# The causal mask of the decays: a minimum on VectorE in place of two TensorE matmuls per row spread

## The reference, cut to what matters

```python
a_cum = jnp.cumsum(a_dt, axis=-1)
causal = jnp.tril(jnp.ones((SSD_CHUNK, SSD_CHUNK), dtype=bool))
decay = jnp.exp(jnp.where(causal, a_cum[..., :, None] - a_cum[..., None, :], -jnp.inf))
cb = jnp.einsum("bclgn,bcsgn->bgcls", cc, bc)
y_diag = jnp.einsum("bgecls,bcsgep->bclgep", cb[:, :, None] * decay, x)
```

## Time and profile before

| what | value |
|---|---|
| time, median of 3 runs | 1684.83 us (1681.4, 1684.83, 1687.41) |
| span of the profiled execution, first to last instruction | 1680.5 us |
| TensorE busy | 1591.5 us, 95% |
| VectorE busy | 1020.3 us, 61% |
| ScalarE busy | 843.9 us, 50% |
| GpSimd busy | 64.0 us, 4% |
| mean granted TensorE clock | 0.985 of full |
| bytes moved | 265.47 MB, 158 GB/s |

### The profile page before, as it was taken

How to read it: one execution, slowest core, us unless ns; L and a number is a source line. 1 busy time by engine, 2 the same in 40 slices (tenths; PEclk the granted TensorE clock), 3 DMA queues, 4 the chain that set the end, 5 groups by cost and what they waited for, 6 DMA issues and landing times.

```text
span 1680.5 us, 21488 instructions
## 1 busy us (share of the span) xinstructions
PE 1591.5 (95%) x8006; PEld 1329.4 (79%) x8006; DVE 1020.3 (61%) x1287; ACT 843.9 (50%) x940; POOL 64.0 (4%) x38
## 2 busy tenths in 40 slices
PE   5999999999999998999999999989999799879987
PEld 4988878788778886988888878778888688668876
DVE  5977765555564544777775655565453665666564
ACT  4556566454444443556666544354433545554463
POOL 0001100000000000010110000000000010001000
PEclk9999999999999999999999999999999899989999
DMA  5443444344445554443334444435555553436341
GB/s 198 154 171 129 149 154 164 133 154 148 170 162 189 187 183 144 151 175 132 144 129 172 151 151 151 150 128 207 195 179 183 194 189 112 157 113 223 113 165 66
DMA packets 39666, 265.47 MB, mean 158 GB/s; under 512 B 4343, under 2 KB 5400, under 8 KB 9112
## 3 DMA queue, kind: packets, MB, share of 16 engines
q1 hardware_dynamic: 37800, 260.41, 42.9%
q10 hardware_dynamic: 1776, 3.83, 0.6%
HBM read 262.39 MB, written 1.84 MB: 157 GB/s over the span
## 4 chain that ended last, share of the span: by engine, by line
PE 84%; DVE 5%; issue 5%; ACT 5%; DMA 1%; ACTq 0%; DVEq 0%; SPq 0%
PE ps L524 22%; PE ps L526 21%; PE ps L525 21%; PE ps L529 4%; PE ps L753 3%; PE ps L754 3%; PE ps L755 3%; ACT w_high L965 2%; DVE scratch L1326 2%; PE ps L634 2%; ACT w_high L1155 1%; PE ps L668 1%; DVE w_low L1326 1%; PE ps L609 1%; PE ps L607 1%
## 5 line engine op out<-in xcount | busy, mean ns | idle before, releaser
L1326 DVE TENSOR_TENSOR w_low<-w_raw,w_high 128x2048 fp32r<-128x2048 f32 (+2 forms) x252 | 559.4, 2226 | 530.6 <-ACT w_high L965 453.1
L965 ACT ACTIVATE w_high<-w_raw 128x2048 fp32r<-128x2048 f32 (+1 forms) x198 | 372.4, 1883 | 428.3 <-PE ps L526 416.3
L524 PE MATMUL ps<-w_high,u_high 128*128 128x512 f32 x1376 | 553.8, 402 | 9.8 <-DVE u_low L1326 5.2
L526 PE MATMUL ps<-w_high,u_low 128*128 128x512 f32 x1376 | 540.0, 392 | 0.0
L525 PE MATMUL ps<-w_low,u_high 128*128 128x512 f32 x1376 | 539.8, 392 | 0.0
L524 PEld LDWEIGHTS ps<-w_high,u_high 128*128 128x128 f32 x1376 | 260.8, 190 | 68.2 <-issue 9.1
L526 PEld LDWEIGHTS ps<-w_high,u_low 128*128 128x128 f32 x1376 | 260.6, 189 | 56.3
L525 PEld LDWEIGHTS ps<-w_low,u_high 128*128 128x128 f32 x1376 | 261.1, 190 | 53.1 <-issue 1.9
L524 PE MATMUL ps<-w_high,b_high 128*128 128x512 f32 x384 | 151.7, 395 | 1.9 <-issue 1.9
L526 PE MATMUL ps<-w_high,b_low 128*128 128x512 f32 x384 | 149.7, 390 | 0.0
L525 PE MATMUL ps<-w_low,b_high 128*128 128x512 f32 x384 | 149.5, 389 | 0.0
(11 more groups left out here) (222 smaller groups left out, 1400.4 us busy)
## 6 DMA issues: line engine op xcount, KB each, us to landing
w_raw<-in_stream SPq DMA_DIRECT2D x238, 1024.0 KB, 4.8
w_raw<-in_stream SPq DMA_DIRECT2D x10, 512.0 KB, 3.4
par<-in_pars SPq DMA_DIRECT2D x4, 265.0 KB, 4.9
h<-in_x SPq DMA_DIRECT2D x1, 1024.0 KB, 7.4
ple_gain<-in_ple_g ACTq DMA_DIRECT2D x2, 512.0 KB, 6.2
scratch<-rev ACTq DMA_DIRECT2D x2, 512.0 KB, 5.6
w_raw<-in_stream SPq DMA_DIRECT2D x4, 256.0 KB, 2.6
out<-h SPq DMA_DIRECT2D x2, 512.0 KB, 2.6
```

The costliest lines, as they stand in the source:

```text
L524: nc.tensor.matmul(o, hi, whi, start=start, stop=False, **kw)
L526: return nc.tensor.matmul(o, lo, whi, start=False, stop=stop, **kw)
L965: nc.scalar.activation(WH[:, c % RING, 0:n], W[:, c % RING, 0:n], ACT.Copy).then_inc(high_ready, 1)
L1326: return nc.vector.tensor_tensor(out=o, in0=a, in1=b, op=op)
```

## The change

The mask matmuls go, and with them the two matrices ident_r and never_r that GpSimd prepared at the start. The spread now sums all 128 rows of decay_rows, with weights that are one in the 64 rows of chunk t and zero in the others. VectorE then takes the minimum of the spread and the running sum of s into EM, and ScalarE takes the exponentials from EM to EM. Where l comes before s the running sum of l is the larger, the minimum is that of s, the exponential is 1, and cb's zero removes it. TensorE's waits for banks 6 and 7 (the state matmul and the off-diagonal product) are now for the minimum and not for the exponentials; VectorE takes over ScalarE's waits. Its minimum stands after the products of x at 2i+7 and, at 2i+9, after what the same chunk number holds for earlier groups.

```diff
@@ TensorE, at c = 2i+6 and 2i+8
-                            k = slice(t * 2 * HEADS, (t + 1) * 2 * HEADS)
-                            ones = tri_r[k, P - 1:P].to_broadcast([2 * HEADS, P])
+                            half_of = (tri_r, later_r)[t][:, P // 2 - 1:P // 2].to_broadcast([P, P])
                             for b in range(2):
-                                nc.tensor.matmul(four(ps[:, 6 + b, :]), ident_r[:, :], bc(never_r[:, :].unsqueeze(1), 4, P),
-                                                 start=True, stop=False)
-                                last = nc.tensor.matmul(ps[:, 6 + b, :], ones, DR[k, b * 512:(b + 1) * 512],
-                                                        start=False, stop=True)
+                                last = nc.tensor.matmul(ps[:, 6 + b, :], half_of, DR[:, b * 512:(b + 1) * 512],
+                                                        start=True, stop=True)
                             last.then_inc(row_ps.sem, 1)
                     if c == 2 * i + 7:
                         pe.wait_ge(xds_ready.sem, xds_ready.at(l, g + 1))
-                        pe.wait_ge(ssd_exp.sem, ssd_exp.at(l, 2 * g + 1))
+                        pe.wait_ge(row_clipped.sem, row_clipped.at(l, 2 * g + 1))
@@ TensorE, at c = 2i+10
-                        pe.wait_ge(ssd_exp.sem, ssd_exp.at(l, 2 * g + 2))
+                        pe.wait_ge(row_clipped.sem, row_clipped.at(l, 2 * g + 2))
@@ ScalarE
                         for t, at_c in ((0, 2 * i + 7), (1, 2 * i + 9)):
                             if c == at_c:
-                                act.wait_ge(row_ps.sem, row_ps.at(l, 2 * g + t + 1))
-                                if g:
-                                    act.wait_ge(yd_ps.sem, yd_ps.at(l, 2 * (g - 1) + t + 1))
+                                act.wait_ge(row_clipped.sem, row_clipped.at(l, 2 * g + t + 1))
                                 for e in range(HPG):
                                     a = t * HEADS + g * HPG + e
-                                    ins = nc.scalar.activation(EM[t][:, e, :], ps[:, 6 + e // 4, tok(e % 4)], ACT.Exp,
+                                    ins = nc.scalar.activation(EM[t][:, e, :], EM[t][:, e, :], ACT.Exp,
                                                                bias=nacum[:, a:a + 1])
@@ GpSimd, at the start
-            nc.gpsimd.tensor_copy(ident_r[:, :], ident)
-            nc.gpsimd.tensor_scalar(never_r[:, :], later, NEG, None, ALU.mult)
@@ VectorE
+                        for t, at_c in ((0, 2 * i + 7), (1, 2 * i + 9)):
+                            if c == at_c:
+                                dve.wait_ge(row_ps.sem, row_ps.at(l, 2 * g + t + 1))
+                                if g:
+                                    dve.wait_ge(yd_ps.sem, yd_ps.at(l, 2 * (g - 1) + t + 1))
+                                tt(EM[t], ps[:, 6:8, :].rearrange("p b (e l) -> p (b e) l", e=4),
+                                   bc(acum[:, t * HEADS + g * HPG:t * HEADS + (g + 1) * HPG].unsqueeze(2), HPG, P), ALU.min)\
+                                    .then_inc(row_clipped.sem, 1)
```

More of the change, by code:

```diff
@@ L162, in build @@
         later_r = nc.alloc_sbuf_tensor_at("later_r", [P, P], F32R, offset=con_at + K_LATER * 4)
-        ident_r = sb("ident_r", [P, P], F32R)
-        never_r = sb("never_r", [P, P], F32R)
         dtw_h = sb("dtw_h", [P, KD * HEADS], F32R)
@@ L372, in build @@
         ssd_m = signal("ssd_m", 2 * GROUPS)
+        row_clipped = signal("row_clipped", 2 * GROUPS)
         ssd_y = signal("ssd_y", 2 * GROUPS)
```

## The result

The changed kernel takes 1692.36 us (median of 5 runs, 1691.97 to 1695.21) against 1686.72 of the kernel before (5 runs, 1681.4 to 1687.45). The ratio over all runs is 1.0043 (the two medians alone give 1.0033), 95% interval [1.0031, 1.0055]: slower, and just measurably so. By the medians the change costs 5.6 us, where the forecast had 3. The forecast of 1687.5 was 4.9 us too low; 1.9 of these are the kernel before, which takes 1686.72 in five runs where three gave 1684.83. The range, 1679 to 1695, held the time, but the likeliest outcome given was "the same".

What follows compares the result with a forecast made beforehand. Bound by equal TensorE and VectorE chains. Groups summed to +2.1 us a layer, clock-corrected to +1.5, +3 for both: 1683.5 of span from 1680.5, or 1687.5 against the median; range 1679 to 1695.

Steps and rivals of the forecast that it cites:

- Saved on TensorE: In the 16 spreads: two 128-row matmuls replace four slower ones, saving 1.2 us a spread, 19.2 us in all (12 to 20).
- Rival E: On TensorE, the new matmuls keep 0.42 each, so only 0.75 a spread is saved: 1684 to 1692 us; chance 0.10.
- Two chains of equal length: Exponential to y takes VectorE 20.8 us, TensorE needs 20.9 meanwhile; the change shortens one chain and lengthens the other.
- rival C: VectorE's chain has unseen slack, so TensorE's saving arrives: 1665.6 us with all 19.2, 1678 with a third; chance 0.10.
- Prices of the minimum and the exponentials: On VectorE 1.21 us per 128x1024 minimum (1.14 behind another instruction); on ScalarE eight exponentials from SBUF 0.25 longer.
- b_low held by decay_rows: Second spread: GpSimd's decay_rows starts between two b_low and holds the second; exponentials 2.25 us late, y 2.5 later.
- rival B: VectorE isn't held: b_low gets in first or GpSimd waits its turn; -1.7 us a layer, 1681.5; chance 0.18.
- rival D: In group 0, GpSimd holds the minimum itself: 3.3 us more over both layers, 1691 to 1696; chance 0.20.
- The sizes by group: Per layer: group 0 -0.5 us, groups 1 and 2 +2.5 each, group 3 -2.4, together +2.1 before the clock correction.
- The term that was mis-sized is group 2: After 4.9 us idle TensorE's clock falls, rows come too late to meet b_low: group 2 costs +1.25, not +2.5.
- The correction for the clock: Half clock for 3.3 us costs TensorE 1.7: layer +0.85 if in group 2, +3.8 if in group 3; taken +1.5.
- Nothing else moves: Outside the stage no time changes; GpSimd's two dropped casts at the start ended long before TensorE's first work.

Runs made afterwards that it cites:

- experiment 1: Against the kernel before: spreads sum 128 rows instead of 64; mask matmuls and exponentials from PSUM stay, no minimum. 1674.83 us against 1686.04.
- Experiment 2: Against the kernel before: only the minimum on VectorE and exponentials from SBUF; 64-row sums and mask matmuls stay. 1696.53 us against 1686.04.
- experiment 8: The changed kernel run again with no edit, for a second profile. 1693.64 us against 1683.09 of the kernel before, one run each.
- Experiment 3: Against the changed kernel: GpSimd starts decay_rows only after the second minimum. 1690.49 us against 1686.04 of the kernel before.
- experiment 4: Experiment 3, and VectorE's split of the chunk after y waits until GpSimd has gated y. 1687.36 us against 1686.04 of the kernel before.
- experiment 5: Against the changed kernel: the second spread's minimum stands ahead of the b_low pair of the group before. 1675.24 us against 1684.72 of the kernel before.
- experiment 6: Experiment 4, and 8 idle-filling matmuls into free bank 6 ahead of TensorE's wait for y. 1684.08 us against 1684.72 of the kernel before.
- experiment 7: Against the changed kernel: second spreads get mask matmuls and exponentials from PSUM back, first keep the minimum. 1671.72 us against 1684.72 of the kernel before.

## Why the prediction was right in kind and short in size

- **Saved on TensorE, 1.2 a spread: right.** From 196.28 to the second chunk matmul at 196.98 it is 0.70 where it was 1.94, 1.24 saved. The cause given stands: experiment 1 changed nothing but the 64 rows to 128, and the matmuls went from 0.42 to 0.23 apart. By the section Tiling Modes of TensorEngine Tiling (Array Packing) in the Trainium skill, a change of mode drains the engine; the trace agrees, with 0.19 to 0.2 a matmul as its price here. Rival E (0.42 kept) falls.
- **Two chains of equal length: right.** TensorE waits for y before groups 1 to 3 of the changed kernel, 4.62 where 4.9 was forecast, and rival C (slack in VectorE's) falls. Experiment 2 shows it without anything else: 1.58 us a group for an instruction of 1.22 and 0.25 of exponentials.
- **Prices of the minimum and the exponentials: right.** Groups by line of the kernel after, over 80 to 275 us for the second (busy us, mean ns, idle before):

```profile
L1318 DVE TENSOR_TENSOR ssd_decay<-ps,small 128x1024 f32<-128x1024 f32 x16 | 19.5, 1220 | 3.3 <-PE ps L605 3.3
...
L1078 ACT ACTIVATE ssd_decay<-ssd_decay,small 128x128 f32<-128x128 f32 x64 | 19.6, 389 | 27.5 <-DVE ssd_decay L1318 27.5
```

  1.22 against 1.21 forecast; eight exponentials in 2.45 against 2.18, 0.27 more where 0.25 was taken.
- **b_low held by decay_rows: right, with both its ends.** The held one of a pair takes 2.36 to 2.42 us, alone it takes 0.69; mostly it was the first, once the second, as forecast. It happened in three of the four places of the first trace and in all four of experiment 8; the escape of rival B was seen once, by 0.03 us, and group 2 was 2.30 longer even so. Experiment 3 prices it at 1.7 in group 1.
- **The minimum itself is not held: right.** 1.23 beside decay_rows at 103.35, so rival D falls. The GPSIMD Engine Reference of the Trainium skill, section Specifications, has contention for two SBUF inputs; the trace agrees with 1.23 for one of each memory and 2.4 for b_low, 0.69 when free.
- **The sizes by group.** Group 0 -0.73 (forecast -0.5), group 1 +2.29 (+2.5), group 3 -2.5 or -0.9 (-2.4 or -0.7, by whether the clock falls there): all near the forecast in the first trace. In experiment 8 group 3 is +0.16.
- **The term that was mis-sized is group 2.** The forecast said that a fall of the clock ahead of it makes the rows come too late to meet b_low, "and that group costs +1.25 instead of +2.5". It measured +2.30 with the clock down and b_low free, and +4.05 in layer 1 and +3.7 in experiment 8 with b_low held too. The step behind it is in the prediction's first spread: it let x·dt end a fixed 9.34 us after the transposes of x, as at 171.48 to 180.82. After, it ends 11.05 later, at 183.97 for 172.92. Where TensorE idles for over 2 us before the transposes, ScalarE has rounded the next chunk before y is done (w_high ends at 170.25, the add of y at 172.78), while in group 0 w_low still waited for it, 0.49 us. So VectorE starts w_low 0.24 before the gating of y, and the gating stands still until it is done: 4.26 instead of 2.38, and with it everything that waits for it. It returned as 4.26 to 4.31 after groups 1 and 2 in both layers of the changed kernel and of experiments 3 and 8, and not after group 0 (idle 1.63), nor in experiments 4 to 7 (2.35 to 2.4), where the order was forced, or the idle time was at most 1.63. That the rows do miss b_low behind a fall came true in one of four cases only: in layer 0 of the first trace.
- **The correction for the clock.** Half clock is real in the stage and cost 1.7, as taken from the earlier trace rows. But it was counted by itself, when it runs beside the held gating: in experiments 3, 4 and 6 group 2 lasts 46.87 with the gating held, 47.03 with the clock down, 46.84 with both and 45.33 with neither. Forecast was +1.5 a layer; the ledger has +1.36 and +4.74, and in experiment 8 +5.44 twice. Three of these four lie above 3.8, the dearest layer that the forecast allowed. That the time still fell into the range owes something to the range's width and to what moves outside the stage.
- **"Nothing else moves": true of the code, not of single executions.** In both attention stages there is a gap of 2.36 between two starts, the same in every kernel. The clock fell behind both in the changed kernel and in experiments 2 and 4, behind one in 3, 5, 6 and 7, and behind none in the kernel before and in experiments 1 and 8. The same kernel has it both ways (the changed one and experiment 8). From the end of the stage in layer 1 to the end of the kernel, where all run the same instructions, the ten traces take 769.5 to 776.2 us, 771.3 before and 776.2 after. Why the clock falls in one execution and not in the other stays open; it moves single spans by as much as the error of the forecast.
- **The base: misread.** The forecast added 4.3 us to a span of 1680.5 to come to the median. These 4.3 are no fixed distance between span and time, which is at most 2.0, but show that the profiled execution was a short one. And 1683.5 and 4.3 make 1687.8, not 1687.5.

## What to carry to other kernels

If the chain of waits names one engine for all of a stretch, measure how long before its use the other engines' last result is ready; at 0.1 us, as here, work moved to them cost its full length at once. Look at where in the queue a new instruction goes, before at its price: the same minimum one place earlier turned +5.6 us into -9.5. An operation on VectorE that reads two SBUF tensors and one on GpSimd, let go by the same event or nearly so, collided here, and the one that came second paid; give them different events, or an order. And look at several executions before a difference of a few microseconds is put down to the edit: one trace each gave 12.9 us where the medians gave 5.6.

## What the runs showed of the hardware that was not expected

- GpSimd and VectorE held each other for about the rest of the other's instruction, in both directions, by who started first: b_low went from 0.69 to 2.4 behind a decay_rows started 0.05 before; the gating from 2.38 to 4.26 behind a w_low started 0.24 before; w_low from 2.28 to 4.20 behind a gating started 0.33 before (at 126.18 in the changed kernel; it cost nothing there, the next group lasts 45.40 with it in experiment 3 and without it in experiment 4); decay_rows from 1.90 to 2.42 behind a b_low started 0.03 before.
- A matmul of 64 rows among those of 128 costs its neighbour as much as itself: 0.42 to 0.43 instead of 0.23 for three of the four, 0.33 for the first, and 11.2 us in the kernel.
- TensorE's clock after idle time, in the ten traces, by the gap between two starts: up to 1100 us, behind gaps of up to 2.08 us it never fell to its lower level of 1.2 GHz; behind 2.36 in 10 of 20 cases; behind 2.62 not in the one case; before the transposes of x behind 3.1 to 3.3 in 5 of 7 and behind 4.4 to 5.0 in 8 of 8; and behind the 3.21 later in layer 0 (470.66 to 473.87 in the kernel before) in 8 of 10. At these places it stayed down for 3.4 or 6.8 us, and each 3.4 cost 1.67 where TensorE was the bound.
